# Head 0's xm projection split by tokens and by tile, small statistics with an operand in PSUM

## What is computed

```python
def rmsnorm(x, g):
    return x * lax.rsqrt(jnp.mean(x * x, axis=-1, keepdims=True) + EPS) * g
# first block ends, second block begins
x  = rms_norm(x, final_g)
h  = rmsnorm(x,   norm_g[0]) * (1.0 + sc)  + sh      # 512 latents
hc = rmsnorm(ctx, norm_g[0]) * (1.0 + scc) + shc     # 256 context tokens
# mlstm_inputs, for h (on an 8 x 64 grid) and for hc (on a 1 x 256 grid)
xm, o_pre, z = jnp.split(hmod @ w_in, 3, axis=-1)    # xm: 2048 channels, 4 heads of 512
xconv = jax.nn.silu(conv3x3_depthwise(xm) + conv_b)
q = xh @ w_q ; k = xh @ w_k * 512 ** -0.5 ; v = xm   # per head
gates = q @ wq_g + k @ wk_g + v @ wv_g
```

## Time and profile before

| | us |
|---|---|
| time before, median of 3 runs | 2626.94 |
| lowest and highest of the 3 | 2623.47, 2627.46 |
| span of the profiled execution | 2622.8 |
| TensorE busy | 2523.2 (96%) |
| GpSimd busy | 1508.8 (58%) |
| VectorE busy | 1240.2 (47%) |
| ScalarE busy | 738.8 (28%) |
| MLP phase ends, mLSTM inputs begin | about 1602.7 |
| head 0's projection on TensorE | 1620.4 to 1655.5 |

### The profile page before, as it was taken

How to read it: one execution, slowest core, us unless ns; L and a number is a source line. 1 busy time by engine, 2 the same in 40 slices (tenths; PEclk the granted TensorE clock), 3 DMA queues, 4 the chain that set the end, 5 groups by cost and what they waited for, 6 DMA issues and landing times. The chain is left out here.

```text
span 2622.8 us, 37081 instructions
## 1 busy us (share of the span) xinstructions
PE 2523.2 (96%) x15074; PEld 2007.2 (77%) x15074; DVE 1240.2 (47%) x1876; ACT 738.8 (28%) x1419; POOL 1508.8 (58%) x758
## 2 busy tenths in 40 slices
PE   5999989999999999999999998999999999999998
PEld 5777677788888796657888886888776578877787
DVE  7736337675562141443444426976484633131212
ACT  5643332331120211452312212333323422011210
POOL 4764633577777665206888873633272057755674
PEclk9999988999999999999999998999999999999999
DMA  6321424666662221203556532322344354221221
GB/s 276 104 81 57 129 80 162 272 240 225 239 225 97 88 105 65 71 1 130 198 215 219 211 118 81 137 98 112 124 158 151 105 222 180 98 92 65 80 97 64
DMA packets 89904, 358.84 MB, mean 137 GB/s; under 512 B 27288, under 2 KB 41112, under 8 KB 52384
## 3 DMA queue, kind: packets, MB, share of 16 engines
q1 hardware_dynamic: 64992, 227.66, 24.1%
q10 hardware_dynamic: 24768, 129.12, 13.1%
HBM read 317.68 MB, written 39.06 MB: 136 GB/s over the span
## 5 line engine op out<-in xcount | busy, mean ns | idle before, releaser
L519 POOL TENSOR_TENSOR whi<-wraw,con_sb 128x512 fp32r<-128x512 f32 (+1 forms) x306 | 625.5, 2063 | 966.5 <-PE ps L575 692.9
L523 POOL TENSOR_TENSOR wlo<-wraw,whi 128x512 fp32r<-128x512 f32 (+1 forms) x306 | 799.6, 2632 | 12.9
L575 PE MATMUL ps<-hh,whi 128*128 128x512 f32 x952 | 372.1, 391 | 0.0
L575 PE MATMUL ps<-hl,whi 128*128 128x512 f32 x952 | 370.5, 389 | 0.0
L575 PE MATMUL ps<-hh,wlo 128*128 128x512 f32 x952 | 370.4, 389 | 0.0
L575 PEld LDWEIGHTS ps<-hh,whi 128*128 128x128 f32 x952 | 178.7, 188 | 41.7 <-issue 4.6
L575 PEld LDWEIGHTS ps<-hh,wlo 128*128 128x128 f32 x952 | 178.7, 188 | 37.4
L575 PEld LDWEIGHTS ps<-hl,whi 128*128 128x128 f32 x952 | 178.7, 188 | 36.6
L575 PE MATMUL ps<-midh,whi 128*128 128x512 f32 x512 | 200.2, 391 | 0.0
L575 PE MATMUL ps<-midl,whi 128*128 128x512 f32 x512 | 199.9, 391 | 0.0
L575 PE MATMUL ps<-midh,wlo 128*128 128x512 f32 x512 | 199.7, 390 | 0.0
(11 more groups left out here) (487 smaller groups left out, 4741.9 us busy)
## 6 DMA issues: line engine op xcount, KB each, us to landing
wraw<-wst SPq DMA_DIRECT2D x162, 1024.0 KB, 4.8
cond_w<-wcond ACTq DMA_DIRECT2D x68, 1024.0 KB, 4.8
first_w<-wcond SPq DMA_DIRECT2D x8, 1024.0 KB, 19.3
mod_w<-wcond SPq DMA_DIRECT2D x8, 1024.0 KB, 14.0
d_v<-key_and_query ACTq DMA_DIRECT2D x4, 1536.0 KB, 5.1
d_s<-ssb ACTq DMA_DIRECT2D x4, 1536.0 KB, 5.3
sld<-d_s SPq DMA_DIRECT2D x4, 1536.0 KB, 8.1
vld<-d_v SPq DMA_DIRECT2D x16, 384.0 KB, 3.5
```

The costliest lines, as they stand in the source:

```text
L519: o = pool.tensor_tensor(whi[:, s, c], wraw[:, f, c], C("zero").broadcast_to([P, width]), ALU.add)
L523: o = pool.tensor_tensor(wlo[:, s, c], wraw[:, f, c], whi[:, s, c].bitcast(F32), ALU.subtract)
L575: o = e.matmul(ps[:, b, :nt], w[:, k, mc], x[:, k0 + k, t0:t0 + nt], start=first and k == 0 and j == 0, stop=final and k == nk - 1 and j == 2)
```

## The change

It changes the order of work at the seam, and where six small operands lie:

- lat_gain moves from the mLSTM phase to the end of the second MLP phase's VectorE work.
- The mean of the final squares (L3003, L3005) and the reciprocal (L3009) are written to columns 8 to 15 of PSUM bank 7, and not to stat2. So each product has one operand in PSUM.
- Head 0's projection is taken apart: the context of block one by tile as the context is parted (both channel tiles in one bank), with the spread of stat2 before tile 2; then qk_product(15); the context of block two; fold_product(15); the latents of block one by tile, with fold_turn before tile 5 and the spread of stat before tile 7; then the latents of block two.
- The context tiles of two channel tiles share one bank, so `order` has six entries for head 0, and ScalarE reads such a bank in one operation of 128 x 512.
- ScalarE's list moves its read-outs between other tiles of h: the qk one behind the first latent tile, the fold one behind the fourth, the turned one behind the sixth.

The diff, cut to its core:

```diff
@@ end of the second MLP phase, VectorE
+                    if layer:
+                        dve.wait_ge(*VE.last())
+                        dve.tensor_tensor(lat_gain[:], coef[:, 5], V("final"), ALU.mult).then_inc(*VE.up(chain))
@@ mLSTM inputs
-        order = [("xm", 0, n) for n in range(8)]
+        order = [("xm", 0, n) for n in (0, 4, 1, 3, 5, 7)]
@@ TensorE
-                fold_product(pe, 14, 0)
-                qk_product(pe, 15, 1)
-                pe.wait_ge(*inverted2.at(1))
-                for to, sp_, of in ((7, spread2, stat2[:, 2]), (6, spread, stat[:, 1])):
-                    if to == 6:
-                        fold_product(pe, 15, 0)
-                        pe.wait_ge(fold_read, 16)
-                        fold_turn(pe, 15, 1).then_inc(fold_made, 1)
-                        pe.wait_ge(*scaled.at(KT))
                     for t in range(4):
                         o = pe.matmul(ps[:, to, P * t:P * t + P], of[:, t:t + 1].broadcast_to([P, P]), ident, start=True, stop=True)
                     o.then_inc(*sp_.inc())
-                pe.wait_ge(fold_read, 17)
-                xm_of(0)
+                def passes(to, j, m, k, part, begins):
+                    wh, wl = (w[:, (first + j) % SPL].rearrange("p (k c) -> p k c", k=KT)[:, k, P * m:P * m + P] for w in (whi, wlo))
+                    for n, (w, x) in enumerate(((wh, h2h), (wh, h2l), (wl, h2h))):
+                        o = pe.matmul(to, w, x[:, k, part], start=begins and n == 0, stop=k == KT - 1 and n == 2,
+                                      skip_group_check=True)
+                    return o
+                def first_context(j):
+                    pe.wait_ge(w_split, first + j + 1)
+                    for k in range(KT):
+                        if j == 0:
+                            if k == 2:
+                                pe.wait_ge(*inverted2.at(1))
+                                spread_columns(7, stat2[:, 2], spread2)
+                            pe.wait_ge(*parted.at(k + 1))
+                        for m in range(2):
+                            o = passes(ps[:, j, TX * m:TX * m + TX], j, m, k, CX, k == 0 and m == 0)
+                            if j == 0 and k == 0 and m == 0:
+                                o.then_inc(w_used, 1)
+                    o.then_inc(*PE.up(acc_ready))
+                def first_latents():
+                    for k in range(KT):
+                        if k == 5:
+                            pe.wait_ge(fold_read, 16)
+                            fold_turn(pe, 15, 6).then_inc(fold_made, 1)
+                        if k == 7:
+                            pe.wait_ge(fold_read, 17)
+                            spread_columns(6, stat[:, 1], spread)
+                        pe.wait_ge(*parted.at(KT + k + 1))
+                        for m in range(2):
+                            o = passes(ps[:, 2 + m], 0, m, k, LAT, k == 0)
+                            if k == KT - 1:
+                                o.then_inc(*PE.up(acc_ready))
+                fold_product(pe, 14, 2)
+                first_context(0)
+                pe.wait_ge(fold_read, 15)
+                qk_product(pe, 15, 3)
+                first_context(1)
+                pe.wait_ge(*scaled.at(KT))
+                fold_product(pe, 15, 6)
+                first_latents()
+                made[0] = turn["acc"] = 4
+                block_of(pe, first + 1, 0, h2h, h2l, KT, 256, tokens=((TX, T),), bank_free=bank_free)
@@ ScalarE
+                def first_tiles():
+                    for j in range(2):
+                        b = bank()
+                        act.wait_ge(*AC.need(acc_ready))
+                        act.activation(xms[0][:, 2 * j:2 * j + 2, CX], ps[:, b].rearrange("p (m t) -> p m t", m=2),
+                                       ACT.Copy).then_inc(*AC.up(acc_taken))
+                    for m in range(4):
+                        read_out(xms[0][:, m, LAT], T)
-                act.activation(stat2[:, 1], stat2[:, 0], ACT.Sqrt, bias=C("epsn")).then_inc(*rooted2.inc())
-                for n in range(2):
+                act.activation(stat2[:, 1], ps[:, 7, 8:12], ACT.Sqrt, bias=C("epsn")).then_inc(*rooted2.inc())
+                fold_read_out(act, 14, 2)
+                for n in range(KT + 1):
                     round_h(n)
-                qk_read_out(act, 15, 1)
-                for n in range(2, 4):
+                qk_read_out(act, 15, 3)
+                for n in range(KT + 1, KT + 4):
                     round_h(n)
-                fold_read_out(act, 15, 0)
+                fold_read_out(act, 15, 6)
+                for n in range(KT + 4, KT + 6):
+                    round_h(n)
                 act.wait_ge(fold_made, 17)
-                turned_read_out(act, 15, 1)
-                for n in range(4, 2 * KT):
+                turned_read_out(act, 15, 6)
+                for n in range(KT + 6, 2 * KT):
                     round_h(n)
@@ VectorE
-                dve.scalar_tensor_tensor(stat2[:, 0], ps[:, 7, 4:8], 1.0 / D, stat[:, 1], ALU.mult, ALU.mult).then_inc(*mean_made.inc())
+                dve.scalar_tensor_tensor(ps[:, 7, 8:12], ps[:, 7, 4:8], 1.0 / D, stat[:, 1], ALU.mult, ALU.mult).then_inc(*mean_made.inc())
-                dve.tensor_tensor(stat2[:, 0], stat2[:, 0], stat[:, 1], ALU.mult).then_inc(*mean_made.inc())
-                dve.tensor_tensor(lat_gain[:], coef[:, 5], V("final"), ALU.mult).then_inc(*gain_made.inc())
+                dve.tensor_tensor(ps[:, 7, 8:12], ps[:, 7, 8:12], stat[:, 1], ALU.mult).then_inc(*mean_made.inc())
-                dve.reciprocal(stat2[:, 3], stat2[:, 1]).then_inc(*gain_made.inc())
-                dve.tensor_tensor(stat2[:, 2], stat2[:, 3], stat[:, 1], ALU.mult).then_inc(*inverted2.inc())
+                dve.reciprocal(ps[:, 7, 12:16], stat2[:, 1]).then_inc(*gain_made.inc())
+                dve.tensor_tensor(stat2[:, 2], ps[:, 7, 12:16], stat[:, 1], ALU.mult).then_inc(*inverted2.inc())
```

More of the change, by code:

```diff
@@ L2258, in _ @@
                                     cond_block(dve, n)
+        stat2, lat_gain = fixed("stat2", [P, 4, 4]), fixed("lat_gain", [P, KT])
         mlp_phase(0, 1)
@@ L2677, in program @@
         LAT = slice(TX, TA)
-        stat2, lat_gain = fixed("stat2", [P, 4, 4]), fixed("lat_gain", [P, KT])
         d_keep = nc.dram_tensor("d_keep", (P, KT, T), F32, kind="Internal").ap()
@@ L2812, in xm_of @@
                 def xm_of(h):
[L2813 to L2816, removed]
                     for m in range(4):
@@ L2821, in xm_of, with spread_columns @@
                             turn_values(h - 1, n)
-                fold_product(pe, 14, 0)
-                qk_product(pe, 15, 1)
-                pe.wait_ge(*inverted2.at(1))
-                for to, sp_, of in ((7, spread2, stat2[:, 2]), (6, spread, stat[:, 1])):
-                    if to == 6:
-                        fold_product(pe, 15, 0)
-                        pe.wait_ge(fold_read, 16)
-                        fold_turn(pe, 15, 1).then_inc(fold_made, 1)
-                        pe.wait_ge(*scaled.at(KT))
+                first = firsts["xm0"][1]
+                def spread_columns(to, of, sp_):
                     for t in range(4):
@@ L2920, in _ @@
                 root(act, rooted)
-                fold_read_out(act, 14, 0)
                 act.wait_ge(*mean_made.at(2))
-                act.activation(stat2[:, 1], stat2[:, 0], ACT.Sqrt, bias=C("epsn")).then_inc(*rooted2.inc())
-                for n in range(2):
+                act.activation(stat2[:, 1], ps[:, 7, 8:12], ACT.Sqrt, bias=C("epsn")).then_inc(*rooted2.inc())
+                fold_read_out(act, 14, 2)
+                for n in range(KT + 1):
                     round_h(n)
-                qk_read_out(act, 15, 1)
-                for n in range(2, 4):
+                qk_read_out(act, 15, 3)
+                for n in range(KT + 1, KT + 4):
                     round_h(n)
-                fold_read_out(act, 15, 0)
+                fold_read_out(act, 15, 6)
+                for n in range(KT + 4, KT + 6):
+                    round_h(n)
                 act.wait_ge(fold_made, 17)
-                turned_read_out(act, 15, 1)
-                for n in range(4, 2 * KT):
+                turned_read_out(act, 15, 6)
+                for n in range(KT + 6, 2 * KT):
                     round_h(n)
-                for m in range(4):
-                    xm_tile(0, m)
+                first_tiles()
                 for m in range(2):
@@ L3002, in _ @@
                 dve.wait_ge(*inverted.at(1))
-                dve.scalar_tensor_tensor(stat2[:, 0], ps[:, 7, 4:8], 1.0 / D, stat[:, 1], ALU.mult, ALU.mult).then_inc(*mean_made.inc())
+                dve.scalar_tensor_tensor(ps[:, 7, 8:12], ps[:, 7, 4:8], 1.0 / D, stat[:, 1], ALU.mult, ALU.mult).then_inc(*mean_made.inc())
                 dve.wait_ge(*mean_made.at(1))
-                dve.tensor_tensor(stat2[:, 0], stat2[:, 0], stat[:, 1], ALU.mult).then_inc(*mean_made.inc())
```

(8 more changed lines are left out.)

## The result

The changed kernel takes 2631.17 us, median of 16 runs, against 2625.72 for the kernel before in the same comparison: ratio 1.0024, 95% interval 1.0017 to 1.0030, so 5.5 us slower between the medians and some 6 by the ratio. The forecast of 2631.0 lies on the median, and in part by luck: it started from 2626.94, the median of the three runs shown, which is 1.2 us above the median of the sixteen, and added a change of 4.1.

The account below looks back on a forecast made before the run. It took VectorE's chain from conv(0, 0) to the hand-over at head 0's first score product as the bound; span 2622.8 + 4.1 = 2626.9, plus 4.1 from span to median, gave 2631.0 us, range 2627.0 to 2635.0.

Parts of the forecast that it names:

- first projection matmul: TensorE's start on head 0's projection, put near 1605.5 us, 15 us earlier than before.
- x_final starts: VectorE's eight operations making x_final, put at 1636.5 us against 1629.67 before, set by TensorE's order of work.
- conv(0, 0): Head 0's first convolution on VectorE, put at 1642.7 us against 1638.6 before, +4.1, without waiting for xm tiles.
- wait for the split, its end: TensorE waiting 6.9 us for GpSimd's split of head 1's next block, up to 1673.2 us, losing its lead.
- wait at the hand-over, its end: TensorE waiting 3.1 us for VectorE's last low part at head 0's first score product, up to 1711.7 us.
- The statistics: L3005 and L3011 on VectorE falling from 2.92 and 2.58 us to 0.16 each, 2.76 and 2.42 us gone.
- TensorE's programme: TensorE's work from 1605.5 us to x_final, summed to 31.0 us, with a 0.9 us stall behind the fold turn.
- the end moves by +4.1: VectorE sets the hand-over at 1711.7 us, and its shift of +4.1 us carries to the end of the kernel.
- rival (a): TensorE's clock: later rise before x_final costs 1.7 us, fall behind the hand-over wait 1.7 more; 2632.7 to 2634.4; chance 0.22.
- Rival (b): No slow stretch or no stall in TensorE's programme: x_final at 1633.3, +0.9, 2627.8 us; chance 0.15.
- (d): The statistics still wait for GpSimd, head 0 starts 2.7 to 5 us later: +7 to +9 us; chance 0.05.
- Rival (c): TensorE's 6.6 us of lead reach the end because VectorE's chain does not set the hand-over: 2620.3 us; chance 0.08.

Follow-up runs that it names:

- order_only: Changed kernel with the statistics products back in SBUF, the new order on TensorE and ScalarE kept; ratio 1.0039 against the kernel before.
- pe_plus: Changed kernel with 18 extra 512-column passes (4.1 us, thrown away) on TensorE between the latents of blocks one and two; ratio 1.0026 against the kernel before.
- stats_only: Kernel before with the statistics part alone (products in PSUM, gain moved to the MLP phase), old orders kept; ratio 0.9997 against the kernel before.
- early_spread: Changed kernel with the fold turn and the spread of x's statistics moved ahead of the latents, turned read-out earlier too; ratio 1.0007 against the kernel before.
- late_fold: Changed kernel with qk product, fold product and turn behind block one's latents, x's spread right behind block two's context; ratio 0.9984 against the kernel before.
- latents_first: late_fold with TensorE taking the latents of block one ahead of the context of block two; ratio 0.9970 against the kernel before.
- late_fold_fill: late_fold with ten extra 512-column passes (2.3 us, thrown away) ahead of head 0's wait for q's last low part; ratio 0.9977 against the kernel before.
- dve_plus: Changed kernel with five more MEMSETs of gacc on VectorE between x_final and conv(0, 0); ratio 1.0041 against the kernel before.

## Why the prediction was right, step by step

Positions after, less the 2.26 us by which this execution was late from the start:

| step | predicted | after |
|---|---|---|
| first projection matmul | 1605.5 | 1605.3 |
| x_final starts | 1636.5 | 1636.3 |
| conv(0, 0) | 1642.7 | 1642.5 |
| wait for the split, its end | 6.9, 1673.2 | 6.8, 1672.9 |
| wait at the hand-over, its end | 3.1, 1711.7 | 2.6, 1711.6 |

**The statistics** fell to 0.17 and 0.16 as taken from L3003. The estimate of 0.065 us more per operation with a PSUM source, from the table in the Trainium skill ("VectorE: DVE Perf Modes", section on the TRN2 errata), isn't seen: the products that now read PSUM take 0.171 and 0.161, and the nearest product with both operands in SBUF and no wait, L3006 with eight columns, 0.155. (The third operation that I counted, the reciprocal, reads SBUF and writes PSUM, for which the table's two figures don't stand; it takes 0.173, before 0.169.) That two SBUF operands wait for GpSimd is shown by order_only, with the same 2.92 us. The Trainium skill ("SBUF — State Buffer", "Who interferes with whom") says that a VectorE instruction with two SBUF inputs contends with a GpSimd instruction that reads SBUF, and that one with at most one SBUF input, outside the modes that use two ports, doesn't; the trace agrees, also for the MEMSET beside the split, 0.70 us.

**TensorE's programme** was right to 0.2 us, with the clock's rise where it was taken and the stall behind the fold turn (0.70 us shown, 0.9 predicted). The three stops of VectorE, with the spread late behind them, were in it: 5.17, 1.56 and 4.28 us, where I had put some 3, some 2 and no figure for the third; the first was hidden all the same. One term was right by accident: between the split and the hand-over I had added 1.8 us to TensorE's 33.6 for banks held by ScalarE. The trace after shows no such wait there, but a slow stretch over 5.6 us of work, and TensorE needs 36.1 us. In pe_plus, without that stretch, the waits for ScalarE are there (1.4 us) and it needs 35.4.

**What was mis-sized is the carry to the end.** The prediction put "the end moves by +4.1", the shift of the hand-over. The hand-over moved by 3.9, but the end by 6.6 in the profile, and the time by 5.5 between the medians. What the sum left out shows in the two stretches behind the hand-over, each with the time in it at which TensorE was granted 1.2 GHz (us):

| kernel | hand-over to last score product | slow in it | last score product to end | slow in it |
|---|---|---|---|---|
| before | 185.6 | 0 | 729.5 | 24.8 |
| after | 187.2 | 3.4 | 730.6 | 27.9 |
| stats_only | 185.6 | 0 | 729.5 | 24.6 |
| order_only | 187.2 | 3.4 | 730.5 | 27.8 |
| early_spread | 188.2 | 5.7 | 730.5 | 27.6 |
| late_fold | 187.2 | 3.4 | 730.5 | 27.5 |
| latents_first | 185.6 | 0 | 728.3 | 21.2 |
| late_fold_fill | 185.6 | 0 | 729.5 | 24.9 |
| pe_plus | 187.2 | 3.4 | 733.5 | 34.4 |
| dve_plus | 187.0 | 3.1 | 729.5 | 24.5 |

The first missing term is the second half of rival (a), the slow clock behind the longer wait, priced there at 1.7 us: 187.2 instead of 185.6, so 1.6. late_fold_fill shows the cause. I had given this a place among the rivals and it belonged in the sum; it put the time beyond the 0.2% that tells slower from the same, which I held less likely than the same. The other half of (a), a later rise of the clock before conv, did not come about. The second missing term is 1.1 us behind the last score product. The table shows that this part, too, follows the slow time in it, kernel by kernel; that is a comparison of ten profiles and no run took it apart, and why the slow time there differs from kernel to kernel is open. The forecast came out nearer than these terms leave room for because its start was 1.2 us too high.

Rival (b), no stall and no slow stretch, is excluded by the trace, (d) by the 0.17 us. Rival (c), that the lead counts, is refuted by pe_plus.

## What to carry to other kernels

A busy engine's early start is worth only what the next hand-over lets through: find the engine that arrives last there, follow its list back, and see which of its waits the new order puts behind more work. Where a read-out or a small spread has others queued behind it, place it by who waits for it, not by where its operands are free: moving the product pieces and one spread made 10.5 us of difference between the changed kernel and late_fold, at the same work. A wait of TensorE can cost a second time behind itself, as the 2.6 us here, which came to 4.2 in full-speed work; look at the granted clock behind each wait that your change lengthens, and don't go by the length of the wait.

## What the hardware showed

- At the hand-over a wait of 1.2 us (before, stats_only) left the clock at 2.4 GHz. Waits of 2.6 us (after, order_only, late_fold) and of 3.2 to 3.3 (dve_plus, pe_plus) were followed by a slow stretch that cost 1.4 to 1.6 us up to the last score product; the 3.3 us of early_spread by a longer one that cost 2.7 (188.2 us, against 185.6). At the split a wait of 2.7 us (pe_plus) left the clock up and one of 2.0 us (early_spread) did not. The cost goes with the slow time behind the wait, somewhat under half of it, and the length of the wait alone decides neither.
- I had cited the Trainium skill ("TensorE: Matmul & The Clock Gate", Part 1) for slow stretches that fall differently on the work from run to run. Over the first 1600 us, which are the same work in all ten profiles, this is seen: the time at 1.2 GHz ahead of the first reciprocal adds up to anything from 54.6 to 75.1 us. At the seam it is not: the clock fell 0.1 to 0.4 us behind the first reciprocal, although that operation lay anywhere from 1600.3 to 1605.3 us, and rose 6.9 to 7.3 us behind it, except in order_only, where TensorE's first projection matmul came 2.6 us later and the clock rose 10.6 us behind the reciprocal.
